# Gate rows and twelve conv tiles by seven block products instead of eight, and a new order of the front of a hybrid decoder layer

## What is computed

```python
h = rms_norm(x, norm_pre)                       # (1024, 1024)
proj = h @ w_in
hq, hf, hi, hg, gqkv, gz, ga, gb = split(proj)  # q, f, values, gate | q k v of the delta heads, gate, decays
f = lb + (1.0 - lb) * sigmoid(hf)
o_a = hgrn2_chunked(silu(hq), 1.0 - f, hi, log f)
qkv = silu(causal_dwconv(gqkv, gdn_conv))       # 12 tiles of 128 channels, 4 taps
q, k = l2_normalize(q), l2_normalize(k)
o_g = gated_delta_chunked(q, k, v, log_a, beta) # solves a unit triangular system in each chunk
mix = concat(norm(o_a) * silu(hg), norm(o_g) * silu(gz)) @ w_out
# then residual, gated MLP with conv, per-layer embedding
```

## Time and profile before

| | us |
|---|---|
| median of three runs | 1424.34 (1424.33 to 1425.36) |
| span of the profiled execution | 1422.4 |
| PE busy | 1410.8 (99%) |
| DVE busy | 1027.0 (72%) |
| ACT busy | 705.3 (50%) |
| POOL busy | 221.3 (16%) |

### The profile page before, as it was taken

How to read it: one execution, slowest core, us unless ns; L and a number is a source line. 1 busy time by engine, 2 the same in 40 slices (tenths; PEclk the granted TensorE clock), 3 DMA queues, 4 the chain that set the end, 5 groups by cost and what they waited for, 6 DMA issues and landing times.

```text
span 1422.4 us, 19769 instructions
## 1 busy us (share of the span) xinstructions
PE 1410.8 (99%) x7235; PEld 1187.2 (83%) x7235; DVE 1027.0 (72%) x1522; ACT 705.3 (50%) x1309; POOL 221.3 (16%) x239
## 2 busy tenths in 40 slices
PE   9999999999999999999999999999999999999998
PEld 7877888888889999888888888888888888888886
DVE  7594545561149887368988999999999576577567
ACT  6443456422258887258663443343345444454455
POOL 4000001101038785010000000000000245300000
PEclk9999999999999999999999999999999999999999
DMA  9442424545623342545442334334327755424213
GB/s 277 68 74 30 45 82 122 148 111 121 152 82 100 118 119 83 207 133 186 126 126 82 119 122 145 114 109 149 119 89 250 247 191 194 139 82 134 89 60 148
DMA packets 153247, 181.00 MB, mean 127 GB/s; under 512 B 21241, under 2 KB 92095, under 8 KB 153152
## 3 DMA queue, kind: packets, MB, share of 16 engines
q1 hardware_dynamic: 153152, 179.74, 43.1%
HBM read 130.43 MB, written 49.28 MB: 126 GB/s over the span
## 4 chain that ended last, share of the span: by engine, by line
PE 94%; DVE 3%; ACT 2%; issue 1%; DMA 0%; DVEq 0%; SPq 0%; ACTq 0%
PE psum L2456 9%; PE psum L2457 9%; PE psum L2458 9%; PE psum L2395 5%; PE psum L2397 5%; PE psum L2396 5%; PE psum L1373 4%; PE psum L674 4%; PE psum L676 4%; PE psum L675 4%; PE psum L2368 4%; PE psum L2369 4%; PE psum L2370 4%; PE psum L734 3%; PE psum L732 3%; PE psum L733 3%
## 5 line engine op out<-in xcount | busy, mean ns | idle before, releaser
L166 DVE TENSOR_TENSOR w_wlo<-w_raw,w_whi 128x1024 fp32r<-128x1024 f32 x66 | 87.4, 1325 | 228.3 <-ACT w_whi L151 228.2
L151 ACT ACTIVATE w_whi<-w_raw 128x1024 fp32r<-128x1024 f32 x66 | 69.7, 1058 | 175.1 <-PE psum L2370 77.1
L3189 DVE TENSOR_TENSOR g_slot<-w_raw,g_slot 128x512 fp32r<-128x512 f32 x77 | 67.6, 878 | 59.1 <-ACT g_slot L2763 59.1
L674 PE MATMUL psum<-h_hi,w_whi 128*128 128x512 f32 x256 | 100.7, 393 | 0.0
L2763 ACT ACTIVATE g_slot<-w_raw 128x512 fp32r<-128x512 f32 x77 | 48.7, 632 | 104.8 <-PE psum L2397 99.7
L676 PE MATMUL psum<-h_hi,w_wlo 128*128 128x512 f32 x256 | 99.8, 390 | 0.0
L675 PE MATMUL psum<-h_lo,w_whi 128*128 128x512 f32 x256 | 99.7, 390 | 0.0
L3447 POOL TENSOR_TENSOR mixed_home<-mixed_home 128x512 f32<-128x512 f32 x11 | 14.7, 1339 | 508.3 <-DMA mixed_home<-in_w_down 505.0
L2368 PE MATMUL psum<-w_whi,m_hi 128*128 128x512 f32 x224 | 87.8, 392 | 0.0
L2370 PE MATMUL psum<-w_whi,m_lo 128*128 128x512 f32 x224 | 87.2, 389 | 0.0
L2369 PE MATMUL psum<-w_wlo,m_hi 128*128 128x512 f32 x224 | 87.2, 389 | 0.0
(11 more groups left out here) (446 smaller groups left out, 3995.8 us busy)
## 6 DMA issues: line engine op xcount, KB each, us to landing
w_raw<-in_w_up SPq DMA_DIRECT2D x39, 512.0 KB, 3.9
w_raw<-in_w_in SPq DMA_DIRECT2D x36, 512.0 KB, 6.7
s_rows<-pair_work SPq DMA_DIRECT2D x11, 1024.0 KB, 4.1
w_raw<-s_rows SPq DMA_DIRECT2D x44, 256.0 KB, 2.6
g_rows<-pair_work SPq DMA_DIRECT2D x18, 512.0 KB, 2.6
w_raw<-g_rows SPq DMA_DIRECT2D x33, 256.0 KB, 3.4
w_raw<-in_w_out SPq DMA_DIRECT2D x16, 512.0 KB, 4.4
mixed_home<-in_w_down SPq DMA_DIRECT2D x32, 256.0 KB, 3.5
```

The costliest lines, as they stand in the source:

```text
L674: pe.matmul(out, wh[:, w], self.hi[:, kt, part], start=(kt == 0), stop=False)
```

## The change

- Values come first (four slabs in `pe_quad`), then gates and columns.
- `Pieces`: the gate rows (two groups of 512 columns) and the twelve conv tiles (six pairs) are multiplied as 2x2 blocks by seven block products for eight (B11, B21, T2, T3, T1, B22, T4). A piece is 12 matmuls: 28 pieces for the rows, 42 for the pairs. Of the sums of blocks that this needs, DVE makes those of h (`dve_form`; ACT and DVE split them), POOL those of the weights (16 for the rows, four in each pair). Partial products are copied out by ACT (`act_pair_copy`) and joined by DVE (L1440).
- The first tap is ACT's (`act_tap`, L1079), squares too; DVE keeps three taps (L1450). The product with beta (a_v, L1624) goes from ACT to DVE. A quarter of h is saved to DRAM and read back before f.
- f now carries all eight chunks, one in each slot of 12 matmuls from slot 1 (`SPREAD`, `F_UNITS`); after each sigmoid (L1224) ACT loads the table of Exp again (L93). q follows at once; no gate rows lie between the chunks and q. `dve_solve` has f's bounds (`dve_open`) and remainders of q's slabs within it. `pe_first_inverse` stands after the heads 2 and 3 of q, before after 1 and 2.

Numbers of instructions on PE: 5174 matmuls of 128x512 become 5102, 96 of 128x256 become none.

```diff
+class Pieces:
+
+
+    RING, AHEAD, PAIRS, QUAD = 4, 3, 3 * NH // 2, KT // 2
+    STEPS = 7
+    B11, B21, T2, T3, T1, B22, T4 = range(STEPS)
+    ROWS = STEPS * QUAD
...
+        self.order = [(0, self.B11)]
+        for p in range(self.PAIRS):
+            self.order += [(p, q) for q in (self.B21, self.T2, self.T3, self.T1)]
+            if p + 1 < self.PAIRS:
+                self.order.append((p + 1, self.B11))
+            self.order += [(p, self.B22), (p, self.T4)]
...
-    STAGES = 3
-    SPREAD = (0, 2, 3, 5, 6, 8, 9, 11)
+    STAGES = 4
+    SPREAD = tuple(range(1, NT + 1))
+    F_UNITS = ((0, 1), (1, 1), (0, 0), (1, 0), (2, 1), (3, 1), (2, 0), (3, 0))
+    SLOTS = 2 * len(F_UNITS)
+    ROUNDED_AT = {5: 2, 7: 3, 13: 4}
...
+            sp.dma_start(part[:, 0:self.QUAD, 0:BANK].bitcast(F32), self.saved[n]).then_inc(s["saved"], 16)
+        self.slabs.load(sp, first["f"] + 3)
+        self.slabs.load(sp, first["q"])
+        for c in range(NT):
+            self.sp_chunk(sp, c)
+            if c in (3, 5):
+                self.slabs.load(sp, first["q"] + 1 + (c == 5))
+        sp.wait_ge(s["lt_stored"], NT * 16)
+        for b in range(P // SB):
+            at = slice(b * SB, (b + 1) * SB)
+            sp.dma_start(self.blk[at, :, :], self.scratch["lt"][at, :, at].rearrange("i g j -> g i j")).then_inc(s["blocks"], 16)
+        self.slabs.load(sp, first["q"] + 3)
         self.slabs.load(sp, first["q"] + NH)
...
+            sp.wait_ge(s["cut"], n + 1)
+            for b in range(P // SB):
+                at = slice(b * SB, (b + 1) * SB)
+                sp.dma_start(self.scratch[name][at, :, at].rearrange("i g j -> g i j"), src[at, :, :]).then_inc(s["x_stored"], 16)
         sp.wait_ge(s["x_stored"], 2 * (P // SB) * 16)
+        for q in (pc.T3, pc.T4):
+            self.banks.released(sp, ("pairs", last, q))
...
+        self.pe_gates(pe)
+        self.pe_quad(pe, 2, 4, NT)
+        self.pe_gate_columns(pe)
+        self.pe_quad(pe, 3, 4, NT)
+        for n in range(pc.ROWS):
+            self.pe_row_piece(pe, n)
+        for p, q in pc.order:
+            if q == pc.B22 and 0 < 2 * p - 1 < 2 * NH:
+                self.pe_sum(pe, 2 * p - 1)
+            if q == pc.T2 and 0 <= 2 * p - 4 < 2 * NH:
+                self.pe_sum(pe, 2 * p - 4)
+            if (p, q) == (pc.PAIRS - 1, pc.B22):
+                self.pe_len_columns(pe)
+                self.pe_cumulate(pe)
+            self.pe_pair(pe, p, q)
+        for i, (h, half) in enumerate(self.F_UNITS):
+            if i == 2:
+                pe.wait_ge(s["saved"], 4 * 16)
+            for two in range(KT // 2):
+                self.pe_turned(pe, "f", h, half, i % 4, half == 0, range(2 * two, 2 * two + 2))
+                slot, late = divmod(4 * i + two, 2)
+                for c in range(NT):
+                    if late and self.SPREAD[c] == slot:
+                        self.pe_chunk(pe, c)
+                    if not late and self.SPREAD[c] + 1 == slot:
+                        self.pe_chunk_turn(pe, c)
...
-        for h in range(NH):
-            for half in range(2):
-                self.pe_turned(pe, "q", h, half, half == 1)
-                if h in (1, 2):
-                    self.scan.pe_first_inverse(pe, 2 * (h - 1) + half)
+                b = self.LAST_BANK if (h, half) == (NH - 1, 1) else (h % 2) * 2 + half
+                self.pe_turned(pe, "q", h, half, b, half == 1, range(KT))
+                if h >= 2:
+                    self.scan.pe_first_inverse(pe, 2 * (h - 2) + half)
         self.n_multiplied = self.multiplied.n
...
+    def pe_pair(self, pe, p, q):
+        pc = self.pieces
...
+        which = 2 if q == pc.B21 else 1 if q in (pc.T3, pc.T4) else 0
+        out = self.banks.open(pe, ("pairs", p, q), 3 * (p % 2) + which)
+        for kt in range(pc.QUAD):
+            w = slice(kt * P, (kt + 1) * P)
+            pe.matmul(out, wh[:, w], hi[:, kt, :], start=(kt == 0 and self.fresh(q)), stop=False,
+                      skip_group_check=not self.fresh(q))
+            pe.matmul(out, wh[:, w], lo[:, kt, :], start=False, stop=False, skip_group_check=not self.fresh(q))
+            ins = pe.matmul(out, wl[:, w], hi[:, kt, :], start=False, stop=(kt == pc.QUAD - 1),
+                            skip_group_check=not self.fresh(q))
+        self.multiplied.mark(ins, ("pairs", p, q), ("front_piece", n))
...
+        tap = self.k.cols[:, C_GCONV + m:C_GCONV + m + 1]
+        act.activation(self.qkv[:, m, :], self.line[u][:, 0:SEQ], ACT.Copy, scale=tap).then_inc(self.s["begun"], 1)
...
+        slabs.round(act, self.first["f"], m_)
+        self.act_silu(act, 2 * last + 1)
+        self.act_tap(act, 2 * last)
+        slabs.round(act, self.first["f"] + 1, m_)
+        self.act_silu(act, 2 * last)
...
+        for slot in range(self.SLOTS):
+            self.act_slot(act, slot)
+            if slot % 2:
+                h, half = self.F_UNITS[slot // 2]
...
+                if slot + 1 < self.SLOTS:
+                    self.banks.released(act, key)
+                    k.table(act, ACT.Exp)
+            if slot in self.ROUNDED_AT:
+                slabs.round(act, first["f"] + self.ROUNDED_AT[slot], m_)
+        slabs.round(act, first["q"] + 1, m_)
...
+            elif q == pc.T4:
+                self.dve_taps(dve, 2 * p + 1)
+        slabs.remainder(dve, self.first["f"])
+        self.dve_pair_join(dve, last, pc.T4)
+        slabs.remainder(dve, self.first["f"] + 1)
+        self.dve_taps(dve, 2 * last)
...
+        for slot in range(self.SLOTS - 5):
+            self.dve_slot(dve, slot)
+            if slot in (5, 7):
+                self.dve_open(dve, (slot - 5) // 2)
+            if slot in self.ROUNDED_AT:
+                slabs.remainder(dve, first["f"] + self.ROUNDED_AT[slot])
...
+        self.dve_solve(dve)
+        slabs.remainder(dve, first["q"] + 2)
...
+        for h in range(NH):
+            dve.wait_ge(s["logged"], h + 1)
+            dve.tensor_tensor_scan(self.f[:, h, :], self.keep, self.f[:, h, :], 0.0, ALU.mult, ALU.add).then_inc(s["summed"], 1)
+        dve.wait_ge(s["summed"], NH)
+        dve.wait_ge(s["x_stored"], 2 * (P // SB) * 16)
+        for lv in range(3):
+            self.scan.dve_differ(dve, 0, lv)
+        slabs.remainder(dve, first["q"] + 3)
+        self.scan.dve_dt(dve, 0, 0)
+        self.scan.dve_dx(dve, 0)
+        slabs.remainder(dve, first["q"] + NH)
+        self.scan.dve_dt(dve, 0, 1)
+
...
+                beta = small[:, 7, c, :].unsqueeze(2).broadcast_to([P, NH, P])
+                self.banks.release(dve.tensor_tensor(self.chunk(2, c), heads(self.banks.of(("a_v", c))), beta, ALU.mult), ("a_v", c))
 
...
         for i in range(SB - 1):
-            if i % 12 == 11:
-                next_slab()
+            if i == 4:
+                slabs.remainder(dve, first["q"])
+            elif i == 7:
+                self.dve_open(dve, 2)
+            elif i == 12:
+                self.dve_open(dve, 3)
+            elif i == 15:
+                slabs.remainder(dve, first["q"] + 1)
```

1046 lines of the change are left out of this document (672 added, 374 removed).

## The result

| | before | after |
|---|---|---|
| median, us | 1424.34 | 1478.51 (1476.72 to 1481.3) |
| ratio | | 1.038 (95% interval 1.0365 to 1.0395) |
| span of the profiled execution | 1422.4 | 1475.0 |

The change made the kernel slower by 54.2 us, or 52.6 by the spans. The forecast was 1447, in a range to 1463: the direction was right, and what PE loses was about 30 us more than forecast, so that the time lies above the range.

A forecast was written before the change was run, and what follows sets the result against it. PE was taken as the bound everywhere: 1424.3 - 27.5 (matmuls) + 9.6 (pairs) + 6.7 (before f) + 14.6 (f) + 15.7 (q) + 3.5 (clock) = 1446.9, taken as 1447 us; range 1414 to 1463.

The forecast's parts named there:

- Matmuls, -27.5: Conv tiles and gate rows: 120 wide matmuls fewer at 0.227 us each, with the 0.3 PE lacked, 27.5 us less.
- rival (d): Row pieces and pairs: a matmul costs more than 0.227 us; at 0.24, 11 us more, 1458 us; chance 0.04.
- Stages taken at nothing: Values, gates and 28 row pieces: ACT, DVE and POOL keep up, nothing added; up to 4 us on the upper side.
- Pairs, 9.6: Conv tile pairs: ACT's and DVE's chain ends after PE wants the sums of lengths; 9.6 us lost, bounds 3 and 15.
- Before f, 6.7: Between pairs and f: PE waits 6.7 us for f's first slab, behind factors and taps; bounds 4 and 8.
- f, 14.6: f with all chunks: late remainders and stores, mainly at slots 5 and 7; 14.6 us lost, bounds 8 and 18.
- q, 15.7: In q: PE waits for x of chunk 0 through solve, cut, stores and reads; 15.7 us lost, bounds 11 and 20.
- The scan as before: The scan behind the front was to run as before, with nothing added.
- Clock, 3.5: PE's clock falls to its lower level once, 3.5 us lost, between none and three falls.
- rival (c): The clock falls in each of five long waits, 17.5 us for 3.5: 1461 us; chance 0.12.
- Rival (a): Queues give way: pairs, transition and f lose 5 us together, q 11; faster, 1412.8 us; chance 0.20.
- Rival (b): All terms come near their low bounds: 1421 to 1430 us; chance 0.12.

The follow-up runs named there:

- experiment 4: Kernel after the change, with POOL's 16 sums for the gate rows cut to 8 of 512 columns (gate rows not the reference's): 1469.75 us, ratio 1.0313.
- experiment 9: Kernel after the change, with three of POOL's four sums in each pair cut to 8 of 512 columns (results not the reference's): 1473.87 us, ratio 1.0354.
- Experiments 2: Kernel after the change, with f's first slab rounded and its remainder made ahead of the last factors and taps: 1480.66 us, ratio 1.039.
- 7: Kernel with three reorderings and q's remainders later in the solve, plus f's first slab ahead of the factors and pe_first_inverse one unit later: 1458.0 us, ratio 1.0236.
- 10: Kernel reordered in f, rows, solve and squares, plus f's first slab ahead, all chunks one slot later and q's loads after chunks 4 and 6: 1453.51 us.
- Experiment 3: Kernel after the change, with 154 small products of ones added in PE's long waits before f, at chunks 5 and 7 and at y32: 1473.09 us.
- the kernel of 12: Kernel with f's reordering, halved remainders of h's sums and the solve's later q remainders, with all weight sums moved from POOL to DVE: 1442.0 us, ratio 1.0125.
- experiment 1: Kernel after the change, with q's second and third slab loaded behind the stores of chunks 4 and 6 instead of ahead: 1465.59 us, ratio 1.0283.
- experiment 5: Kernel after the change, with f's opens, remainders and q's loads later, h's sum remainders in halves, and odd sums of lengths one piece later: 1460.9 us.

## Where the prediction was right and where it failed

- **What bounds, and the side.** PE's matmuls count in full, and the waits outweigh them: right. The five places named have their waits, with the releasers named.
- **Matmuls, -27.5.** The spacing in the pieces is 0.226, so rival (d), costlier products, falls.
- **Stages taken at nothing: failed.** The step "DVE one remainder (0.68)" took DVE's price from the kernel before, where POOL seldom worked beside it, and "POOL's 16 sums are done well within 76 us" looked only at POOL's end. Each sum held up what DVE began beside it until it was done, by up to 1.1 us. The bound of 4 upward was too narrow: 6.3 in waits, 8.8 in time (experiment 4). The trace of before did show it, in a stage that I had not read for this, the MLP: in its timeline a remainder that starts beside an operation of POOL takes 1.64 and ends 0.55 after it, and the shortest of the 77 of that line take 0.68.

```profile
1154.63 1.64 DVE L3189 TENSOR_TENSOR g_slot<-w_raw,g_slot 128x512 fp32r<-128x512 f32 x1
```

```profile
1154.43 1.29 POOL L3452 TENSOR_TENSOR mixed_home<-mixed_home 128x512 f32<-128x512 f32 x1 [1.51 <-DMA mixed_home<-in_w_down]
```

- **Pairs, 9.6 for 13.0: the chain was right, its DVE prices off.** 2.4, 1.3, 1.3, 4.0 were forecast; without three of POOL's sums 1.1, 1.0, 1.0, 3.8 are left (experiment 9), beside small ones up to 1.8 for banks. To each of three, POOL's sums added 1.8. Without POOL the five would be 8.6 from start to start, near the forecast, but partly by luck: the second pair's 2.4 came as 1.1, and the 1.8 for a bank was not forecast. The decays' tables cost what was forecast. The bound of 15 held.
- **Before f, 6.7: right** at 6.6, through the queue as added up. Experiments 2, 7 and 10 show that it can be moved, not that it can be hidden.
- **f, 14.6: failed in one link.** Counted as the prediction counts, from the end of slot 5's products at 337.2: the remainder ends at 11.9 (forecast 11.7), L1608 starts at 11.8, PE has come to the transposes at 10.3 (10.2). But the bank comes free at 22.6, not 16.2, since "the stores of chunk 4's lt and at, which take 2.6 to land" took 8.8 for at. The order in SP's queue had been seen; the price was that of a store with nothing big before it. Here 512 KB of q's weights are issued 0.4 us ahead of the stores. With it come 11.8 for 6.0 at slot 5 and 10.3 for 6.1 at slot 7 (start to start), 22.3 in all; the bound of 18 was too low. The prediction also weighed a dearer table load, 5.5 more in f, and let the row decide: the row held.
- **q, 15.7 for 13.5: right** in its path, 2.2 high. The solve ended at F + 23.8 (forecast 24.6), and y32 went at F + 40.9 (43.0):

```profile
402.65 1.23 DVE L178 TENSOR_TENSOR w_wlo<-w_raw,w_whi 128x1024 fp32r<-128x1024 f32 x1 [6.05 <-ACT w_whi L163]
...
428.42 0.19 DVE L1648 TENSOR_TENSOR b_blk<-b_blk,b_tmp 128x31 f32<-128x31 f32 x1
```

```profile
445.74 1.94 PE L1834 MATMUL psum<-rows_stage 128*128 128x64 f32 x8 [10.20 <-DMA rows_stage<-lt_rows]
```

- **The scan as before: a small miss**, 2.5 in two waits at its start, which were not looked into.
- **Clock, 3.5: failed; rival (c) had the mechanism.** "I take one fall" became six. All five of the waits that (c) names had one, and the rows one more, but at 1.4 to 2.7 each and not 3.5: (c) put 17.5 for 3.5, and 11.6 came by the estimate above. Experiment 3 won back 5.4 net with some of the waits filled. The windows agree with what the Trainium skill advises on the page "TensorE: Matmul & The Clock Gate", section "Why this matters for your kernels", to leave no idle gaps between bursts: 0.50 behind the wait of 6.4, 1.00 with that wait filled. In the forecast the absence of a row that showed it was read as evidence against it; a kernel whose PE never waits can't have such a row.
- **Rival (a), that the queues give way, falls:** in f and q the remainders came within 1 us of when their queues let them (forecast 11.7, came 11.9; forecast F + 24.6 for the solve, came F + 23.8).
- **Rival (b)** falls with (a): no term but q's came out under its forecast by more than 0.1.
- **The range** ended at 1463 though all high bounds together gave 1472, and three of those bounds, 4, 18 and 10.5, were below what came (6.3, 22.3, 11.6).

Not all adds up exactly. Each cause taken alone gave 12.9 (SP's order), 8.8 (POOL in the rows), 5.95 (POOL in the pairs, on the kernel of 12) and 5.4 (clock, in part), 33 together for the 30 us that the forecast lacked. These overlap: a wait taken away also takes its half-clock stretch along, and I haven't told these apart.

## What to carry to other kernels

Work given to an idle engine is not free to its neighbours: price both engines' operations as they run beside each other, and where one of them has slack, try to let it do both; here 40 operations more for DVE left its busy time as it was and made the kernel 13 us faster. Ahead of each small store that something waits for, look at what the same queue issues before it, and don't take the landing time from a row where nothing did. Where PE goes from no waits to several, count a stretch at the lower clock for each long one (in the kernel after every wait of 3.8 and more had one during or behind it), and before saving matmuls in a stage, list what is done under it.

## What the runs showed of the hardware

- DVE and POOL take turns when both work on two operands in SBUF: the operation that starts second ends a little less than its own time after the first one's end. All 28 remainders of L3189 in the MLP of before that began during an operation of POOL ended 0.55 to 0.64 after it, and 17 of L361 in the front of after 0.55 to 0.57 (alone they take 0.69); POOL's 1.29 sums begun within such an operation of DVE ended 1.12 to 1.16 after it. So DVE's 128x512 went from 0.69 to as much as 1.78, its 128x2048 from 2.28 to 3.38, POOL's 128x512 from 1.29 to 1.75 or 3.3, and the one that began first was not slowed by the later one.
- With one operand in PSUM there were no turns: DVE's joins (L1440) took 0.68, and POOL's five sums begun within them 1.29 to 1.31.
- The issue of the store of at on SP took 2.81 behind the load of q's slab and 0.43 ahead of it (experiment 1); it landed 8.8 after its issue in the one case and 2.35 in the other. The load itself landed after 8.5, and after 8.1 in experiment 1.
- The lower clock came behind waits as short as 2.3 to 2.9 in some places and not in others: at 98 after three of 2.3, at 269 after the wait of 3.8, not after those of 2.9 between, whereas in the kernel of experiment 5 it came after each of the pairs' waits. The stretches measured 3.4, 6.8, 10.2 and 13.7.
- Where it falls behind short waits is not the program's doing alone. The kernels of experiments 1 and 3 are the same up to the last pair and ran on one chip, and yet the profile of the one has five such stretches there and starts the last product of the pairs at 299.4, the other has two and starts it at 295.4. So up to 4 us between two single profiles can be that; and four executions of the kernel after lie 4.6 us apart, four of before 1.3.
